# Second-product expert weights loaded from ScalarE's DMA queue instead of SyncE's

## The reference, cut to what matters

```
hid = silu(h @ e_w1[l, e]) * (h @ e_w3[l, e])      # 1024 -> 512
out += gate * (hid @ e_w2[l, e])                   # 512 -> 1024
```

## Time and profile before

| | |
|---|---|
| median of three runs | 2571.17 us |
| profiled execution, its own time | 2565.58 us |
| span of the profiled execution (first to last instruction) | 2563.8 us |
| TensorE busy | 2301.2 us (90% of the span) |
| ScalarE busy | 565.4 us (22%) |
| queue q1 (SP) | 122600 packets, 388.37 MB |
| queue q10 (ACT) | 11776 packets, 9.97 MB |
| mean granted TensorE clock | 0.950 |

### The profile page before, as it was taken

How to read it: one execution, slowest core, us unless ns; L and a number is a source line. 1 busy time by engine, 2 the same in 40 slices (tenths; PEclk the granted TensorE clock), 3 DMA queues, 4 the chain that set the end, 5 groups by cost and what they waited for, 6 DMA issues and landing times. The chain is left out here.

```text
span 2563.8 us, 34524 instructions
## 1 busy us (share of the span) xinstructions
PE 2301.2 (90%) x14586; PEld 1398.0 (55%) x14586; DVE 824.0 (32%) x1443; ACT 565.4 (22%) x1162; POOL 95.8 (4%) x64
## 2 busy tenths in 40 slices
PE   6999999989988987997689999999999889699875
PEld 3545754664566544554355466547545665455543
DVE  1245612341356223110023654125305561311002
ACT  2132401320155112000021332024201650210000
POOL 0000000000022000000000000001000210000000
PEclk8999998999999998999989999989999999899987
DMA  7222033213411214999942210422143112179995
GB/s 262 95 101 86 1 131 133 83 47 131 164 50 50 89 49 197 379 417 421 406 155 106 72 63 18 180 92 73 66 143 138 56 58 68 43 282 410 421 421 191
DMA packets 136261, 406.89 MB, mean 159 GB/s; under 512 B 9446, under 2 KB 34534, under 8 KB 125352
## 3 DMA queue, kind: packets, MB, share of 16 engines
q1 hardware_dynamic: 122600, 388.37, 39.8%
q10 hardware_dynamic: 11776, 9.97, 1.2%
q0 software_dynamic: 1728, 6.29, 0.7%
HBM read 388.59 MB, written 16.02 MB: 158 GB/s over the span
## 5 line engine op out<-in xcount | busy, mean ns | idle before, releaser
L311 PE MATMUL ps<-hT,ring 128*128 128x384 f32 x1344 | 459.1, 502 | 27.8 <-ACT hT L452 12.9
L311 PEld LDWEIGHTS ps<-hT,ring 128*128 128x128 f32 x1344 | 261.1, 197 | 212.5 <-issue 39.4
L311 PE MATMUL ps<-ring,hT 128*128 128x512 f32 x768 | 337.6, 601 | 3.9 <-PEq L1085 3.9
L311 PE MATMUL ps<-arena,ring 128*128 128x384 f32 x768 | 253.0, 492 | 11.1 <-DVE arena L514 5.1
L311 PEld LDWEIGHTS ps<-ring,hT 128*128 128x128 f32 x768 | 147.2, 193 | 192.6 <-issue 191.9
L311 PEld LDWEIGHTS ps<-arena,ring 128*128 128x128 f32 x768 | 146.9, 192 | 115.4 <-issue 17.1
L1965 PE MATMUL ps<-arena 128*32 128x256 f32 x2432 | 146.5, 403 | 32.4 <-DMA arena<-in_e_w 32.4
L1965 PE MATMUL ps<-ring,arena 128*32 128x256 f32 x2432 | 141.0, 392 | 29.0 <-DMA ring<-in_e_w 24.4
L1965 PEld LDWEIGHTS ps<-arena 128*32 128x32 f32 x2432 | 86.2, 116 | 88.1 <-issue 45.9
L1965 PEld LDWEIGHTS ps<-ring,arena 128*32 128x32 f32 x2432 | 86.7, 113 | 79.8 <-issue 32.1
L343 PE MATMUL ps<-cst,arena 128*128 128x128 f32 x472 | 76.0, 308 | 54.3 <-DVE arena L2264 22.9
(11 more groups left out here) (293 smaller groups left out, 2457.7 us busy)
## 6 DMA issues: line engine op xcount, KB each, us to landing
ring<-in_e_w SPq DMA_DIRECT2D x48, 2048.0 KB, 16.3
arena<-in_e_w SPq DMA_DIRECT2D x48, 2048.0 KB, 17.4
ring<-in_w_in SPq DMA_DIRECT2D x36, 2048.0 KB, 7.9
ring<-in_w_ada SPq DMA_DIRECT2D x24, 2048.0 KB, 8.2
ring<-in_a_wo SPq DMA_DIRECT2D x4, 2048.0 KB, 11.8
ring<-in_b_wo SPq DMA_DIRECT2D x4, 2048.0 KB, 8.1
ring<-in_c_wo SPq DMA_DIRECT2D x4, 2048.0 KB, 8.4
ring<-in_w_out SPq DMA_DIRECT2D x4, 2048.0 KB, 7.8
```

The costliest lines, as they stand in the source:

```text
L311: ins = pe.matmul(out, a, b, start=(i == 0), stop=(i == len(pairs) - 1))
```

## The change

SP no longer waits for y(e-1) and no longer issues w2(e+1) for e+1 from 2 to 15. ACT issues it instead, right after `output(e-1)`, that is behind the copies and the four stores of expert e-1. It reads the expert's number from `order_at` itself. The loads of experts 0 and 1, and everything else, stay.

```
--- before.py
+++ after.py
@@ -2032,9 +2032,6 @@
                             sp.wait_ge(*made(("w13", e, last_bank(e))))
                             load_expert(sp, 0, l, e + 2, held[e + 2])
                             load_expert(sp, 1, l, e + 2, held[e + 2])
-                        if 0 < e:
-                            sp.wait_ge(*made(("y", e - 1, last_bank(e - 1))))
-                            load_expert(sp, 2, l, e + 1, held[e + 1])
                     if l + 1 < DEPTH:
                         sp.wait_ge(*made(("w13", NE - 2, last_bank(NE - 2))))
                         load_weights(sp, l + 1, 0, 2)
@@ -2113,6 +2110,9 @@
                         silu(e)
                         if e:
                             output(e - 1)
+                        if 0 < e < NE - 1:
+                            chosen_expert = act.value_load(order_at[0:1, e + 1:e + 2], min_val=0, max_val=NE - 1)
+                            load_expert(act, 2, l, e + 1, nc.s_assert_within(chosen_expert, 0, NE - 1))
                     output(NE - 1)
                     overflow_act(act)
                     if l + 1 < DEPTH:
```

## The result

The changed kernel takes 2622.38 us (median of 4 runs, 2618.84 to 2623.74), the kernel before 2571.57 us beside it: 1.0208 times as long [1.0194, 1.0222], 51 us. Forecast were +20 us and a range up to 2616. The profiled execution took 2618.84 us, its span 2617.1 us.

The account below looks back on a forecast made before the run. DMA was taken to bound the narrow experts. Gaps of 17.6, layer 0's end +3.9 and layer 1's end -1.8 made +20 us: 2585.6 us profiled, 2591 us as a median, range 2568 to 2616.

Parts of the forecast that it names:

- Turns row by row: Two busy queues sharing a DMA engine alternate single rows, however long; ACT's has 48 rows an expert, SP's 16.
- Rival 4: Several w2 rows go for one w13 row, so w13 lands late; 2578 us, chance 0.12.
- ACT's 1.0 us and the later issue: Per layer ACT's added 1.0 us is hidden by h; w2 issued 3.3 us after y; taken as 0.
- The first late w2 and how often: Narrow experts: y(6) waits 9.6 us; w2 late at 6, 9, 12 and 15; no DMA time by itself.
- the 8 to 18 forecast: Sign: y waits 8 to 18 us for w2 at about every third narrow expert.
- Three to one: SP's queue moves w13 of three experts while ACT's moves stores and w2 of one: late every third expert.
- The gap that costs: Behind a late y in narrow experts, DMA engines stand empty 4.4 us; two gaps a layer, 17.6 us in all.
- The upper bound of 35: Upper bound of the gap term: a gap at every second narrow expert, 4 a layer, 35 us.
- The ends: End of layer 0: slabs ahead of w2(15), partly given back, +3.9 us; end of layer 1: -1.8 us.
- The 9.9: End of layer 0: slabs ahead of w2(15) delay y(15) by 9.9 us, before 6.0 us come back.
- Rivals 2 and 3: 2: nothing lost, 2571 us, chance 0.14; 3: two queues fill the engines better, 2565 us, chance 0.08.
- Rival 1: Gaps at every second expert, TensorE slower after waits: 37 to 51 us, say 2615; chance 0.20.

Follow-up runs that it names:

- e3: Kernel before, SP still loading w2 on its own queue but only after ACT's copies, stores and number read: 2568.96 us, ratio 1.0003.
- e13: e7 with 18 small ScalarE copies and a semaphore wait ahead of the w2 issue, still ahead of the stores: 2602.78 us, ratio 1.0111.
- e7: Changed kernel, but ACT issues w2 right after its copies, ahead of the stores: 2586.72 us, ratio 1.0060.
- e5_again: Second run of the changed kernel with layer 0's three slabs issued only after y(14): 2612.90 us, ratio 1.0179; the first run, e5_again's twin, took 2619.01 us.
- e1: Changed kernel with w2 read as 128 rows of 16 KB, giving another second product: 2574.43 us, ratio 1.0027.
- e4: Changed kernel, but SP issues the stores of experts 0 to 13, leaving little but w2 on ACT's queue: 2572.25 us, ratio 1.0009.
- e12: Changed kernel, but ACT issues w2 of experts 2 to 5 only and SP the others: 2570.70 us, ratio 1.0009.
- e14: Changed kernel with e13's delay put between the stores and the w2 issue, some 5 us after y: 2622.76 us, ratio 1.0196.
- e10: e7 with ten small ScalarE copies and no wait ahead of the w2 issue: 2585.91 us, ratio 1.0078.
- e9: Kernel before with w2 in 16-KB rows and h reading every fourth column of w1 and w3: 2780.49 us, ratio 1.0824.

## Why the prediction was wrong in size

Sign, place and mechanism held; the sum was less than half, 20 us of 51. By its own steps:

- **Turns row by row.** Held, at 186 to 187. Rival 4, with several rows of w2 for one of w13, falls: w2 starves. The Trainium skill ("DMA: Bandwidth & Descriptors", section "Queues, rings and completion order") has bundles of typically 9 to 17 descriptors; these counts show none.
- **ACT's 1.0 us and the later issue.** Free by themselves (e3). With a starved queue the later issue should count, since the gap behind a late y lasts until w2 is out; e13 against e7 points that way without settling it.
- **The first late w2 and how often.** y(6) waited 12.8 us, forecast 9.6. The working has a slip here: from 1128 to 1131 us there is room for 3 / 0.16 = 19 rows of w2, not 25. With 13 rows left beside w13(9) its own figures give 13 x 0.776 = 10.1 us, a landing at 1143.0 and a wait of 14.3 us. Late at 6, 9 and 12 in both layers, by the count of rows; these waits of 12 to 18 us lie in the 8 to 18 forecast. At 15 the count was right by luck: in layer 1 y(15) waited 2.2 us, and the 11.35 us of layer 0 are the slabs', as it waited 1.0 us in e5_again. Three to one needs w13 beside w2(15), and none was left to load.
- **The gap that costs: the step that failed**, 17.6 us forecast, a net 32.0 measured. The two gaps counted, behind y(9) and y(12), were 5.5 to 6.1 us, not 4.4: +5.7 in all. The working let a late y run 3.64 us; it ran 6.28 and 6.52 at the lower clock, and w2 goes out only behind it; this would give 2.6 to 2.9 us more a gap where 1.1 to 1.7 came, and no run tests it. Behind y(6), where "no gap opens", there are 1.9 and 2.0 us. This follows from the slip: with 13 rows of w2 beside w13(9), 3 of its 16 rows were still to come, not 9, and 3 x 0.616 = 1.8 us don't fill a gap of 4.4. In the trace w13(9), issued at 1132.89, had landed at 1149.6, and y(6) ended at 1151.10. And at the end of layer 1 it forgot that the w13 left to load run out: 4.7 and 1.7 us, where before had 2.4. 17.6 + 5.7 + 3.9 + 4.0 = 31.2, nearly the 32.0. The upper bound of 35, a gap at every second expert, has the right size for another reason.
- **Left out of the sum: rows that take longer.** With both queues at work a 4-KB row took 0.166 us instead of 0.161 in layer 1, a 16-KB row 0.635 instead of 0.631, a store's 0.050 instead of 0.046. The working took the bytes for unchanged in cost. Of the 5.9 and 5.0 us in the table some 4.1 and 4.6 are longer rows, the rest rows that lay outside the cuts before.
- **The ends.** Forecast +3.9 in layer 0; the trace has 13.2 of slab rows less 5.8 given back, 7.4, and e5_again 8.8. The 9.9 lacked the third slab, which goes out when y(14) ends at 1281, beside w2(15). Layer 1: -1.8 forecast, -1.3 found behind the landing.
- Together 32.0 + 10.9 + 7.4 - 1.3 = 49.0; with 3.6 ahead of the mixtures and 0.7 that I can't place, the 53.3 between the two executions.

Rivals 2 and 3 fall with the share of 0.93 and 0.87. Rival 1 had 37 to 51 us in price, but not its mechanism: y was late every third time, not every second. Its other half, TensorE slower after a wait, did show (clock 0.57 in the late y); that it cost as part of the gap is argued and not tested.

What is shown: the loss needs the short rows (e1), the stores on the same queue (e4), for most of it ahead of w2 (e7), and the narrow experts (e12), and neither the late issue (e3) nor the second queue (e4) makes it alone. What stays open: the exact share of gaps and of longer rows in the 51 us, and how much a later issue costs in the starved queue. The sums are from one trace, and e14, with longer gaps and the same time, and e5, with a new gap in place of the slabs, say that a gap taken away partly comes back elsewhere.

## What to carry to other kernels

In these runs two busy queues shared the DMA engines row by row, so the one with more rows per unit of work fell behind, whatever the bytes. Before moving a load to another queue, count the rows of one round on each queue, what already stands in it included, and look at what stands ahead of the load that is waited for: 48 rows against 16 lost 2.1% with the stores ahead of w2 and 0.6% with w2 ahead of the stores, 32 against 32 lost nothing. In a stretch bound by DMA look then for the moment in which the favoured queue has run as far ahead as its buffers let it; the time is lost there, not in the wait that the profile lists.

## What the runs showed of the hardware that was not expected

- ScalarE's four stores, issued in 1.75 us, took 16.69 us of its queue in e7 with a w2 just ahead of them. Why is not shown.
- A DMA issue on ScalarE's queue did not wait for copies that stand before it in the program (e10); only a semaphore made it wait (e13).
- Rows of 4 KB in turn with 16-KB ones took 2 to 3% longer than in one queue (0.161 to 0.165 and 0.166 us).
- At the end of a wait of 17.6 us TensorE's granted clock stood at 0.50 (1.2 GHz), and the 64 matmuls behind it took 6.28 us for 3.64.
- fp32 weights read at a step of four elements: 634 ns a matmul for 397 (e9). The Trainium skill ("SBUF — State Buffer", section "Door 1: The DMA port swizzle (why `[64,N]` ≈ `[32,N]`)") says that consecutive accesses to one 16-byte line run at full rate and that each access that crosses to a new line pays for it. Four fp32 elements are 16 bytes, so at this step each access is to a new line, and e9 agrees with that.
